# Neighbourhood attention: softmax sums taken as products of ones with the turned exponents, in place of the exponent's accumulator

## The reference

```python
def neighbourhood_attention(q, k, v, k_c, v_c, rpb):
    ...
        s_w = jnp.einsum('bqhd,biqjhd->bhqij', q_r, kwin).astype(jnp.float32) * scale
        s_w = s_w + jnp.transpose(bias, (0, 2, 1, 3))[None].astype(jnp.float32)
        s_w = s_w.reshape(B, H, GRID_W, kh * kw)
        s_c = jnp.einsum('bqhd,bkhd->bhqk', q_r, k_c).astype(jnp.float32) * scale
        p = jax.nn.softmax(jnp.concatenate([s_w, s_c], axis=-1), axis=-1)
        ...
        return (jnp.einsum('bhqij,biqjhd->bqhd', p_w, vwin.astype(jnp.float32))
                + jnp.einsum('bhqk,bkhd->bqhd', p_c, v_c.astype(jnp.float32)))
```

## Time and profile before

| | us |
|---|---|
| median of 3 runs | 1598.87 |
| lowest, highest | 1598.22, 1600.55 |
| profiled execution | 1599.41 |
| its span, first to last instruction | 1597.6 |
| mean granted clock of PE | 0.990 |

### The profile page before, as it was taken

The page is one execution under the profiler, slowest core; times in us unless marked ns, Lnnn a source line. Parts: engine busy times, 40 slices in busy tenths (PEclk is TensorE's granted clock), DMA queues, the critical chain, the costliest instruction groups (busy, mean ns, idle before and its releaser), DMA issues. The chain is left out here.

```text
span 1597.6 us, 29315 instructions
## 1 busy us (share of the span) xinstructions
PE 1494.8 (94%) x12381; PEld 1265.2 (79%) x12381; DVE 708.5 (44%) x1162; ACT 648.1 (41%) x1034; POOL 406.7 (25%) x106
## 2 busy tenths in 40 slices
PE   4999999888999999999999999978889999999998
PEld 4888897777787878997788988657778888888886
DVE  5344147778745521125544335476545334334002
ACT  5311226766654411117743543552344434434112
POOL 1222221111030233312022332100052444434342
PEclk9999999999999999999999999989999999999999
DMA  9344462244141032148313331000120332231321
GB/s 372 127 159 159 159 185 67 67 107 99 35 159 53 1 125 86 53 142 231 108 53 117 105 120 38 1 1 4 56 95 12 132 105 82 102 105 53 132 100 58
DMA packets 34163, 158.35 MB, mean 99 GB/s; under 512 B 6904, under 2 KB 8440, under 8 KB 19584
## 3 DMA queue, kind: packets, MB, share of 16 engines
q1 hardware_dynamic: 33024, 156.46, 29.6%
q10 hardware_dynamic: 1024, 0.21, 0.1%
HBM read 133.58 MB, written 3.15 MB: 86 GB/s over the span
## 5 line engine op out<-in xcount | busy, mean ns | idle before, releaser
L222 PE MATMUL banks<-ffn_token_parts,ffu_weight_parts 128*128 128x512 f32 (+1 forms) x1056 | 229.6, 380 | 1.2 <-POOL ffu_weight_parts L203 0.9
L222 PEld LDWEIGHTS banks<-ffn_token_parts,ffu_weight_parts 128*128 128x128 f32 x1056 | 191.7, 188 | 39.0 <-POOL ffu_weight_parts L203 1.1
L203 POOL TENSOR_TENSOR even_weight_parts<-weight_chunk,even_weight_parts 128x2048 fp32r<-128x2048 f32 x15 | 70.3, 4685 | 306.4 <-ACT even_weight_parts L197 306.4
L203 POOL TENSOR_TENSOR ffu_weight_parts<-weight_chunk,ffu_weight_parts 128x2048 fp32r<-128x2048 f32 x22 | 101.6, 4618 | 157.6 <-ACT ffu_weight_parts L197 157.6
L222 PE MATMUL banks<-even_token_parts,even_weight_parts 128*128 128x512 f32 (+1 forms) x672 | 124.8, 345 | 0.0
L1005 PE MATMUL banks<-even_token_parts,even_weight_parts 128*128 128x512 f32 (+1 forms) x576 | 121.6, 346 | 0.0
L3253 PE MATMUL banks<-ffd_weight_parts,ffn_f_parts 128*128 128x512 f32 x528 | 120.1, 389 | 1.6 <-PEq L3154 1.6
L222 PEld LDWEIGHTS banks<-even_token_parts,even_weight_parts 128*128 128x128 f32 x672 | 103.5, 188 | 19.5 <-issue 3.8
L3253 PEld LDWEIGHTS banks<-ffd_weight_parts,ffn_f_parts 128*128 128x128 f32 x528 | 99.1, 188 | 22.5 <-issue 2.0
L222 PE MATMUL banks<-sec_token_parts,sec_weight_parts 128*128 128x512 f32 (+1 forms) x528 | 114.8, 375 | 0.3 <-PEq L297 0.3
L3231 DVE SCALAR_TENSOR_TENSOR ffn_conv<-banks,b_ffn_taps,ffn_conv 128x511 f32<-128x511 f32 (+1 forms) x88 | 61.9, 745 | 111.8 <-ACT ffn_conv L3203 108.8
(11 more groups left out here) (458 smaller groups left out, 2673.5 us busy)
## 6 DMA issues: line engine op xcount, KB each, us to landing
weight_chunk<-in_ffn_up SPq DMA_DIRECT2D x22, 1024.0 KB, 4.8
weight_chunk<-in_w_in_even SPq DMA_DIRECT2D x16, 1024.0 KB, 7.1
front_late<-in_w_mod SPq DMA_DIRECT2D x16, 1024.0 KB, 5.0
weight_chunk<-in_w_in SPq DMA_DIRECT2D x13, 1024.0 KB, 4.9
weight_chunk<-in_w_out SPq DMA_DIRECT2D x12, 1024.0 KB, 6.0
weight_chunk<-in_w_in_odd SPq DMA_DIRECT2D x12, 1024.0 KB, 4.9
weight_chunk<-in_ffn_down SPq DMA_DIRECT2D x11, 1024.0 KB, 4.9
front_w<-in_w_mod SPq DMA_DIRECT2D x8, 1024.0 KB, 23.5
```

The source lines that it names most:

```text
L203: (on or self.nc.gpsimd).tensor_tensor(parts[:, 1], self.env.raw[s][:], parts[:, 0].bitcast(F32), ALU.subtract).then_inc(self.lo_done, 1)
L222: m = self.nc.tensor.matmul(o, w, env.tok[:, tp, k, a:b], start=n == 0, stop=n == 3 * KD - 1)
```

## The change

The row sums of the exponents are no longer taken by ACT's accumulator. `ones`, a tile of 128 x 64, is filled by DVE once. In `weigh`, ahead of the value products, PE makes eight products of `ones` with the turned exponents, for the same four tiles of keys and two heads, into the columns that the spread products used. Each of a head's 64 output rows holds the sums of its 128 queries. The two spread products go. DVE takes a reciprocal of the 128 x 128 sums in PSUM into `inverse_sum` (L1861 in the changed kernel), in place of two reciprocals of one column, and then makes the same two multiplications.

```diff
-                    pe.wait_ge(inverted, 2 * n + 2)
-                    for h in range(2):
-                        u = (2 * n + h) % 16
-                        r = nc.tensor.matmul(
-                            env.PS[h * C_HD : (h + 1) * C_HD, at + P : at + 2 * P], recip[:, u : u + 1].to_broadcast([P, C_HD]), env.ident[:],
-                            start=True, stop=True)
-                    r.then_inc(spread, 1)
+                    if n == 0:
+                        pe.wait_ge(ones_made, 1)
+                    for j in range(KT):
+                        for h in range(2):
+                            r = nc.tensor.matmul(
+                                env.PS[h * C_HD : (h + 1) * C_HD, at + P : at + 2 * P], ones[:], exT[(2 * n + h) % 4][:, cols(j)],
+                                start=j == 0, stop=j == KT - 1)
+                    r.then_inc(summed, 1)
                     for j, kt in enumerate((*NA_TILES[n % TX], TX, TX + 1)):
...
                     nc.scalar.activation(
-                        ex[u % 4], scored[u % 2][:], ACT.Exp, bias=neg_max[:, u % 4 : u % 4 + 1], scale=-1.0,
-                        accum_out=sums[:, u % 16 : u % 16 + 1]).then_inc(exp_done, 1)
+                        ex[u % 4], scored[u % 2][:], ACT.Exp, bias=neg_max[:, u % 4 : u % 4 + 1], scale=-1.0).then_inc(exp_done, 1)
...
-                def inverse(u):
-                    dve.wait_ge(exp_done, u + 1)
-                    nc.vector.reciprocal(recip[:, u % 16 : u % 16 + 1], sums[:, u % 16 : u % 16 + 1]).then_inc(inverted, 1)
-
...
                     dve.wait_ge(pv_ready, n + 1)
-                    dve.wait_ge(spread, n + 1)
-                    st.link(nc.vector.tensor_tensor(view, rows(env.PS[:, at + P : at + 2 * P]), view, ALU.mult))
+                    dve.wait_ge(summed, n + 1)
+                    st.link(nc.vector.reciprocal(inverse_sum[:], env.PS[:, at + P : at + 2 * P]))
+                    st.link(nc.vector.tensor_tensor(view, rows(inverse_sum[:]), view, ALU.mult))
                     nc.vector.tensor_tensor(view, rows(env.PS[:, at : at + P]), view, ALU.mult).then_inc(o_out, 1)
 
+                nc.vector.memset(ones[:], 1.0).then_inc(ones_made, 1)
```

More of the change, by code:

```diff
@@ L1732, in stage_neighbourhood @@
         exT = [query_room[:, b * KEYS : (b + 1) * KEYS] for b in range(4)]
-        neg_max, sums, recip = sb("neg_max", [P, 4]), sb("sums", [P, 16]), sb("recip", [P, 16])
+        neg_max, ones, inverse_sum = sb("neg_max", [P, 4]), sb("ones", [P, C_HD]), sb("inverse_sum", [P, P])
         more_bias_in, more_stacked = sem("more_bias_in"), [sem(f"more_stacked{h}") for h in range(2)]
         scores_ready, max_ready, exp_done, turned, turned_out = sem("scores"), sem("max"), sem("exp"), sem("turned"), sem("turned_out")
-        pv_ready, o_out, dve_step, inverted, spread = sem("pv"), sem("o_out"), sem("step"), sem("inverted"), sem("spread")
+        pv_ready, o_out, dve_step, ones_made, summed = sem("pv"), sem("o_out"), sem("step"), sem("ones_made"), sem("summed")
         mixed_hi = sem("mixed_hi")
@@ L1873, in _ @@
                         biased(u)
-                    if u >= 2:
-                        inverse(u - 2)
                     if u >= 7 and u % 2:
```

## The result

| | before | changed |
|---|---|---|
| median of 7 runs, us | 1600.55 | 1610.28 |
| lowest, highest | 1598.22, 1608.38 | 1607.91, 1611.31 |
| span of the profiled execution | 1597.6 | 1606.1 |
| stage: first scores to first product of L385 | 56.34 | 66.82 |

What follows compares the result with a forecast made beforehand. TensorE's issue was taken to bound the stage; 10.4 (rows) + 1.0 (reciprocal) - 0.3 (accumulator reads) - 0.68 (query stack) = +10.4 us, on a base of 1598.87: forecast 1609.3 us, range 1605.5 to 1612.0.

Steps and rivals of the forecast that it cites:

- TensorE's issue is the bound: Neighbourhood stage: TensorE's own issue sets the pace, 3.25 us per pair of units, and work added to its list adds time.
- the row at 766.40 against 766.44: One pair before the change: ScalarE's copy ended at 766.40, PE's turn loads at 766.44, so PE did not wait for data.
- 12 rows at 0.054, 0.65 per pair: Stage's pairs: 16 rows of products added, 4 dropped, at 0.054 us a row; +10.4 us over 16 pairs.
- The bound below of 0.48: Low end of the added time per pair, if the 0.17 us after the spread products went with them; 7.7 us in all.
- The gap of 0.17: TensorE loses 0.17 us going into and out of 64-column products, in both kernels, so the change does not remove it.
- rival (a): The gap belongs to the spread products: 0.48 us per pair, +7.7 us, 1606.6 us; chance 0.10.
- The reads of the accumulator, -0.3: ScalarE's 32 reads go: worth nothing in steady state, -0.3 us while the stage's pipeline fills.
- Rival (b): A ring of waits, not PE's issue, paces the stage: 1600.9 us, or 1596.0 through the accumulator read; chance 0.05.
- The reciprocal, hidden in the loop and +1.0 at the end: VectorE's wide reciprocal, 0.95 us, costs nothing in the loop and +1.0 us behind the last value products.
- Rival (c): VectorE becomes the bound, from a reciprocal of 1.75 us; at 2.2 us the time is 1616.4 us; chance 0.05.
- The late query stack, -0.68: At unit 16 the scores' wait for their query stack goes: -0.68 us, at the least -0.4, at the most 0.
- After the stage everything moves along: Behind the stage: PE runs 24.91 us without idle time, no wait appears, and late work moves with the stage's end.

Runs made afterwards that it cites:

- the run with the reciprocal at the end: The kernel before with one more, unused 128 x 128 reciprocal on VectorE ahead of the last pair's two multiplications; stage 56.64 us.
- two pairs in one group: The kernel before with value and spread products of two pairs in a row at every fourth unit; 0.9995 of before, stage 55.85 us.

## Why the prediction was right, point by point

- **TensorE's issue is the bound.** Right. It rested on the row at 766.40 against 766.44 and on who waits for whom. One tile in the sums gives 3.25 us a pair, four give 3.90, four taken twice give 4.78.
- **12 rows at 0.054, 0.65 per pair.** Right: 0.66 in the change, 0.0547 a row when doubled. 16 pairs give 10.5, where 10.4 was said. The bound below of 0.48 has a slip in its working: the 0.08 in it has no row, and only takes 0.57 back to the 0.65 of the forecast. So 0.48 is 0.65 less one gap; both savings at once would have been 0.40, or 6.4 us in all. The forecast does not use it.
- **The gap of 0.17 is that of the 64-column group.** Right, so rival (a) falls. In the changed kernel it is there without a spread; a second group costs 0.30 more, and a group fewer gives 0.35 back. The rule of the Trainium skill in TensorEngine Tiling (Array Packing), Key Properties, that a change of tiling mode drains TensorE, would have it so, and the three cases agree. They show the price of a group, not the drain itself.
- **The reads of the accumulator, -0.3.** Right: 5.83 to 5.55, and 5.84 when put back. Rival (b) falls with it.
- **The reciprocal, hidden in the loop and +1.0 at the end.** Right: 954 ns, with PSUM as the source, and the stage is 0.95 shorter without it. Rival (c) needed 1.75 us.
- **The late query stack, -0.68.** Right for the one profile, too narrow as a term. The wait is gone in every profile at 3.9 us a pair or slower. But in kernels at 3.25 or faster it was 0, 0.4, 1.7 and 1.9 us on TensorE (by its products' rows), so what the change gives back is not one number. The bounds of 0 and -0.68 held for that profile and not for all. The stack came between 24.9 and 26.1 us after the first scores where it was waited for, and before 24.2 us in the run with the reciprocal at the end, so its arrival differs from one execution to another.
- **After the stage everything moves along.** Here a step failed. "No wait appears" is true, yet the longer idle time ahead of L385 (2.13 for 1.21) was read as 1.0 us and no more. In the first profile the clock fell behind it, for another 1.5 us. Working out the idle time was possible ahead; its effect on the clock had not been thought of.
- **The number itself.** The sum for the stage, +10.4 against 10.48, is no luck: its four terms came out at 10.5, 0.95, -0.28 and -0.68. That 1609.3 lies within 1.0 us of the measured median is in part luck. The base that it was added to, 1598.87, was 1.7 below the median of the seven executions, the 1.5 us of the clock were missing, and the difference of the medians came out 0.7 below the sum.

The sum for the span would then be 10.5 + 1.5 = 12.0, less a part if the query stack is late by more than 0.68 in some executions of the kernel before, as it was in two of the experiments; only one execution of that kernel has a profile, so this is not shown. The medians moved by 9.7 and the interval reaches from 5.3 to 10.9. This is less than the profile's stage and clock together give, and the missing part is within what the untouched parts of the program vary: from L395 to the end they took 774.2 us in the changed kernel's first profile and 780.2 in its second. The granted clock may be one part of that, here from 1040 to 1080 in the first and in the second (columns as above):

```profile
1040.00:1080.00 40.00, 26.81 (x172) 16.62 (x171) 28.70 (x24) 27.34 (x39) 0.00 (x0) 0.96 0.00 0
```

```profile
1040.00:1080.00 40.00, 28.18 (x161) 16.29 (x160) 27.27 (x23) 27.01 (x39) 0.00 (x0) 0.83 0.00 0
```

## What to carry to other kernels

A sum taken off one engine's accumulator is not free on TensorE: price it in rows of the shape that is there already, and check first which engine waits for which. Here two rows of each head, spread from one column, were replaced by eight, on the one engine that was not waiting in the loop, to spare two engines that were. Where 64-column products alternate with full ones, as here, the number of groups has a price of its own (0.30 to 0.35 us each). Where a late transfer is waited for, time saved ahead of it can only lengthen the wait: that took 1.3 of the 2.3 us that two pairs in one group should have saved.

## What was not expected of the hardware

The granted clock fell to 0.50 for some microseconds after TensorE had been idle for 2.13 to 2.20 us at the end of the stage in six of seven profiles, and did not after 1.14 to 1.26 us in five of five. One microsecond more of VectorE's work at a place where TensorE has nothing to do thus came to 2.5 to 3.9 us when it happened. In one execution with 2.13 us it did not happen, and no reason was found; it was the only one with the long idle time on its chip.
